# Operands of the delta chain beside the inverses, last merge in two quadrants, first chunk of the RWKV-7 chain in buffers of its own

## The reference, cut to what matters

```python
# RWKV-7, from a zero state, 8 heads of 64
sa = einsum('bhij,bhj->bhi', s, -kkt)
s = s * wt[:, :, None, :] + sa[..., None] * (kkt * at)[:, :, None, :] + vt[..., None] * kt[:, :, None, :]
y = einsum('bhij,bhj->bhi', s, rt)

# gated delta rule, chunked, from a zero state, 4 heads of 128
tv = triangular_solve(ia, bc[..., None] * vc); tk = triangular_solve(ia, (bc * exp(G))[..., None] * kc)
qk = where(incl, einsum('nbhtd,nbhsd->nbhts', qc, kc) * dmat, 0.0)
u = tvi - tki @ s;  o = (qi * exp(gi)) @ s + qki @ u;  s = exp(gl) * s + (ki * exp(gl - gi)).T @ u
```

## Time and profile before

| | |
|---|---|
| runs | 2246.23 us median (2241.65 to 2248.21) |
| profiled execution | 2248.08 us, its span 2246.0 us, mean granted clock of TensorE 0.934 |
| TensorE matmul busy | 2029.4 us (90%) |
| VectorE, ScalarE, GpSimd busy | 1214.4, 497.2, 222.2 us |
| even inverses and RWKV-7 chain | from 320.4 to 383.9 us, and from 384.4 to 466.1 us |
| delta inverses and delta chain | from 1469.0 to 1505.7 us, and from 1506.2 to 1554.1 us |

### The profile page before, as it was taken

One profiled execution on the slowest core, in us unless ns is written; L12 is line 12 of the kernel. 1 busy time (PEld: TensorE's weight loads), 2 busy tenths in 40 slices (PEclk: granted clock), 3 DMA queues, 4 the chain that ended last, 5 costly groups with the idle time before them and its releaser, 6 DMA issues. The chain is left out here.

```text
span 2246.0 us, 40426 instructions
## 1 busy us (share of the span) xinstructions
PE 2029.4 (90%) x17833; PEld 1887.6 (84%) x17833; DVE 1214.4 (54%) x1490; ACT 497.2 (22%) x833; POOL 222.2 (10%) x217
## 2 busy tenths in 40 slices
PE   7998558969988999999999989776699799999999
PEld 6997448859976999999999965465599589999999
DVE  6884655258534655554467445444584355555532
ACT  2221533233222211111011035430422321111000
POOL 3111021013010100000110011011220010000000
PEclk9998767889999999999999989777899999999999
DMA  5221100013562222232222240200244722222321
GB/s 183 86 76 61 38 20 3 1 45 118 171 256 109 94 86 92 93 111 92 79 81 92 93 145 19 84 2 10 99 151 141 299 67 94 93 85 93 109 90 64
DMA packets 52400, 209.10 MB, mean 93 GB/s; under 512 B 6450, under 2 KB 7090, under 8 KB 46258
## 3 DMA queue, kind: packets, MB, share of 16 engines
q1 hardware_dynamic: 52274, 207.30, 26.9%
HBM read 193.88 MB, written 13.40 MB: 92 GB/s over the span
## 5 line engine op out<-in xcount | busy, mean ns | idle before, releaser
L416 PE MATMUL ps<-mx_hi,w_hi 128*128 128x260 f32 x2560 | 521.1, 285 | 16.9 <-DVE w_lo L393 9.7
L416 PE MATMUL ps<-mx_hi,w_lo 128*128 128x260 f32 x2560 | 516.9, 284 | 0.0
L416 PE MATMUL ps<-mx_lo,w_hi 128*128 128x260 f32 x2560 | 516.6, 283 | 0.0
L416 PEld LDWEIGHTS ps<-mx_hi,w_hi 128*128 128x128 f32 x2560 | 396.3, 189 | 21.3 <-DVE w_lo L393 9.9
L416 PEld LDWEIGHTS ps<-mx_hi,w_lo 128*128 128x128 f32 x2560 | 396.3, 189 | 0.0
L416 PEld LDWEIGHTS ps<-mx_lo,w_hi 128*128 128x128 f32 x2560 | 395.4, 189 | 0.0
L391 DVE CAST w_hi<-w 128x1024 fp32r<-128x1024 f32 (+1 forms) x256 | 187.9, 734 | 309.7 <-PE ps L416 302.6
L393 DVE TENSOR_TENSOR w_lo<-w,w_hi 128x1024 fp32r<-128x1024 f32 (+1 forms) x256 | 330.4, 1290 | 8.8
L416 PE MATMUL ps<-hid_hi,w_hi 128*128 128x260 f32 x704 | 141.8, 283 | 0.0
L416 PE MATMUL ps<-hid_hi,w_lo 128*128 128x260 f32 x704 | 141.7, 283 | 0.0
L416 PE MATMUL ps<-hid_lo,w_hi 128*128 128x260 f32 x704 | 141.3, 282 | 0.0
(11 more groups left out here) (490 smaller groups left out, 2834.1 us busy)
## 6 DMA issues: line engine op xcount, KB each, us to landing
w<-in_w_gu SPq DMA_DIRECT2D x88, 512.0 KB, 3.3
w<-in_w_in SPq DMA_DIRECT2D x56, 512.0 KB, 3.3
w<-in_w_down SPq DMA_DIRECT2D x32, 704.0 KB, 4.0
w<-in_w_xkv SPq DMA_DIRECT2D x32, 512.0 KB, 3.4
scr<-in_mem_k SPq DMA_DIRECT2D x10, 1024.0 KB, 6.9
scr<-in_mem_v SPq DMA_DIRECT2D x10, 1024.0 KB, 14.1
w<-in_w_out SPq DMA_DIRECT2D x16, 512.0 KB, 3.3
w<-in_w_xq SPq DMA_DIRECT2D x16, 512.0 KB, 3.4
```

Source lines behind the costliest of these rows:

```text
L416: ins = nc.tensor.matmul(self.ps[:, 2 * (o % 2) + s, 0:b - a], w[:, k, :], v[:, x, a:b], start=first, stop=last)
```

## The change

1. **Delta inverses.** A new class `ChainOperands` does there, in PSUM banks 4 to 7, what the delta chain opened with: TensorE turns the values after `fill` (16 transposes), turns the keys after merge 0 (16 transposes), multiplies keys by queries after merge 2 (16 products). ScalarE copies the turned values (chunks 0 and 1 ahead of merge 0, 2 and 3 behind it), VectorE scales the turned keys after merge 1 (4 instructions) and the products after merge 3 (4 instructions).
2. **Delta chain.** What is left ahead of the first product is the scaling of the inverses by beta, now in two halves. GpSimd scales `k` and then `q` by the decay, both from the stage's start. The copy of the first right side is gone; the scratch offsets are laid out anew.
3. **Last merge.** In TensorE's order L1670 of group n-2 alternates, head by head, with L1663 of group n. With four groups that is two steps with both, with two groups none.
4. **RWKV-7 chain.** Even chunks use what were the odd buffers, cleared by GpSimd in the inverses' stage (`zeroed`); the others are cleared by VectorE behind the masked copies of chunk 0. Chunk 0's transposes and matrices have banks of their own. The two products with the zero state (L1836 and L1869 for t = 0) are left out.

```diff
-    E_INV, E_VT, E_KT, E_QK, E_U, E_S, E_R = 6144, 0, 2048, 4096, 8192, 10240, 12800
+    E_INV, E_VT, E_KT, E_QK, E_U, E_S, E_R = 6144, 8192, 10240, 13408, 0, 3584, 12288
+class ChainOperands:
+    def bank(self, t):
+        return self.k.ps[:, 4 + t, :].rearrange("p (h e) -> p h e", h=4)
+    def keys_turned(self, pe):
+        k = self.k
+        for t in range(NC):
+            pe.wait_ge(k.chain_kept.sem, k.chain_kept.at(t + 1))
+            for h in range(4):
+                ins = k.nc.tensor.transpose(self.bank(t)[:, h], self.keys[:, h, t * P:(t + 1) * P], k.const("ident"))
+            ins.then_inc(k.chain_turned.sem, 1)
+    def keys_scaled(self, dve):
+        k = self.k
+        for t in range(NC):
+            dve.wait_ge(k.chain_turned.sem, k.chain_turned.at(NC + t + 1))
+            decay = self.decay[:, t].unsqueeze(2).to_broadcast([P, 4, P])
+            k.dve.tell(k.nc.vector.tensor_tensor(self.kt[:, t], self.bank(t), decay, ALU.mult), k.chain_scaled)
...
 unit_inverses, TensorE:
                     fill(pe, g, 2 * g)
+                if beside:
+                    beside.values_turned(pe)
...
+                    if beside and n == 0:
+                        beside.keys_turned(pe)
+                    if beside and n == 2:
+                        beside.keys_by_queries(pe)
...
+                for n in range(groups + 2):
+                    first, second = n < groups, n >= 2
...
+                        if first:
+                            ins = nc.tensor.matmul(self.ps[upper, 2 * n, cols], lt[n][lower, h, upper], wide[n][lower, h],
+                                                   start=True, stop=True)
...
+                        if second:
+                            ins = nc.tensor.matmul(self.ps[lower, 2 * n - 3, cols], wide[n - 2][upper, h],
+                                                   inv[n - 2][upper, h, upper], start=True, stop=True)
...
 unit_inverses, GpSimd, ScalarE, VectorE:
+                for t in zeroed:
+                    self.pool.step(nc.gpsimd.memset(t, 0.0))
...
+                if beside:
+                    beside.values_kept(act, range(0, 2))
...
+                    if beside and n == 0:
+                        beside.values_kept(act, range(2, NC))
...
+                    if beside and n == 1:
+                        beside.keys_scaled(dve)
+                    if beside and n == 3:
+                        beside.products_scaled(dve)
...
 rwkv_chain:
+        def token_bank(t, n):
+            return 6 + n % 2 if t else n
+        def matrix_bank(t, n):
+            return 6 if t else 6 - 2 * n
...
-                for out in (ak, rb, rk):
-                    for half in out:
-                        self.dve.step(nc.vector.memset(half, 0.0))
                 self.dve.step(nc.vector.memset(st[:, 0], 0.0))
                 for n in range(3):
                     masked(0, n)
+                for out in (ak, rb, rk):
+                    self.dve.step(nc.vector.memset(out[1], 0.0))
...
 delta_chain, TensorE in the loop, GpSimd, VectorE:
+                        if t == 1:
+                            pe.wait_ge(self.pool_out.sem, self.pool_out.at(1))
...
+                        ins = nc.tensor.matmul(self.ps[:, 5, h * P:(h + 1) * P], inv[:, t, h], rr[:, h] if t else vt[:, 0, h],
+                                               start=True, stop=True)
...
+                for x in (k, q):
+                    self.pool.tell(nc.gpsimd.tensor_tensor(x[:, :, 0:T], x[:, :, 0:T], eg[:, :, 0:T], ALU.mult), self.pool_out)
...
+                for g in range(2):
+                    own = inv[:, 2 * g:2 * g + 2].rearrange("p c h t -> p (c h) t")
+                    beta = col[:, 1, 2 * g:2 * g + 2].rearrange("p c h -> p (c h)").unsqueeze(2).to_broadcast([P, 8, P])
+                    ins = nc.vector.tensor_tensor(own, own, beta, ALU.mult)
+                    self.dve.step(ins) if g else self.dve.tell(ins, self.vector_out2)
```

More of the change, by code:

```diff
@@ L1570, in _, with unit_inverses @@
                 self.dve.tell(nc.vector.tensor_tensor(ss, ss, t2, ALU.add), self.vector_out)
-    def unit_inverses(self, groups, factor, lt_at, uv_at, x_at, ltd_at, xd_at, inv, fill):
+    def unit_inverses(self, groups, factor, lt_at, uv_at, x_at, ltd_at, xd_at, inv, fill, beside=None, zeroed=()):
         nc = self.nc
@@ L1658, in _ @@
                     ins.then_inc(self.tensor_out2.sem, 1)
-                for g in range(groups):
-                    pe.wait_ge(*after(self.vector_out, 2 + n_merge, g))
-                    pe.wait_ge(*after(self.scalar_out2, 0, g))
-                    for h in range(8):
[L1663 to L1672, removed]
+                for n in range(groups + 2):
+                    first, second = n < groups, n >= 2
+                    if first:
+                        pe.wait_ge(*after(self.vector_out, 2 + n_merge, n))
+                        pe.wait_ge(*after(self.scalar_out2, 0, n))
+                    if second:
+                        pe.wait_ge(*after(self.scalar_out, 2 + n_merge, n - 2))
+                        pe.wait_ge(*after(self.pool_out, 2, n - 2))
+                    for h in range(8):
+                        cols = slice(64 * h, 64 * h + 64)
+                        if first:
+                            ins = nc.tensor.matmul(self.ps[upper, 2 * n, cols], lt[n][lower, h, upper], wide[n][lower, h],
+                                                   start=True, stop=True)
+                            if h == 7:
+                                ins.then_inc(self.tensor_out.sem, 1)
+                        if second:
+                            ins = nc.tensor.matmul(self.ps[lower, 2 * n - 3, cols], wide[n - 2][upper, h],
+                                                   inv[n - 2][upper, h, upper], start=True, stop=True)
+                            if h == 7:
+                                ins.then_inc(self.tensor_out2.sem, 1)
                 self.tensor_out.count += (1 + n_merge + 2) * groups
@@ L1829, in _ @@
                         j = h % 4
[L1830 to L1831 removed]
+                        ins = nc.tensor.matmul(self.ps[:, h // 4, j * 64:(j + 1) * 64], ak[x][:, h], vt[x][:, j, h // 4],
+                                               start=j == 0, stop=not t and j == 3, skip_group_check=True)
                     if t:
                         pe.wait_ge(self.vector_out2.sem, self.vector_out2.at(t))
[L1834 to L1837, removed]
+                        for h in self.BY_ROWS:
+                            rows, j = self.head_slot(h)
+                            ins = nc.tensor.matmul(self.ps[:, h // 4, j * 64:(j + 1) * 64], A[rows, j, cols], st[rows, t, j],
+                                                   start=False, stop=j == 3, skip_group_check=True)
                     ins.then_inc(self.tensor_out.sem, 1)
+                    if not t:
+                        pe.wait_ge(self.vector_out.sem, self.vector_out.at(3))
                     for h in range(8):
@@ L1864, in _ @@
                     for h in range(8):
-                        nc.tensor.matmul(out_of(t, h), sa[:, h], rb[x][:, h], start=False, stop=False, skip_group_check=True)
+                        ins = nc.tensor.matmul(out_of(t, h), sa[:, h], rb[x][:, h], start=False, stop=not t and h % 4 == 3,
+                                               skip_group_check=True)
+                    if not t:
+                        ins.then_inc(self.tensor_out.sem, 1)
                     prepare(t + 1, (4,))
[L1867 to L1871, removed]
+                    if t:
+                        for h in self.BY_ROWS:
+                            rows, j = self.head_slot(h)
+                            ins = nc.tensor.matmul(out_of(t, h), st[rows, t, j], R[rows, j, cols], start=False, stop=j == 3,
+                                                   skip_group_check=True)
+                        ins.then_inc(self.tensor_out.sem, 1)
                     prepare(t + 1, (5,))
@@ L2972, in _ @@
             def _(act):
-                act.wait_ge(self.tensor_out.sem, self.tensor_out.at(1))
-                self.act.tell(nc.scalar.activation(wide(vt), self.banks(0, 4), ACT.Copy), self.scalar_out)
                 for t in range(NC):
```

104 lines of the change are left out of this document (54 added, 50 removed).

## The result

The changed kernel's median is **2219.62 us** (2216.16 to 2224.28, four runs) against 2243.95 (2241.65 to 2248.21, four runs): ratio 0.9889, 95% interval 0.9871 to 0.9906. It is 24.3 us faster; 21.8 were forecast, and 2224.4 lies 4.8 above the median, within the range. Of the 4.8, 2.3 are the kernel before itself: the forecast started from its median of 2246.23, here it is 2243.95. The profiled execution took 2224.28, span 2222.1, so against the span of before 23.9 us shorter.

A forecast was written before the change was run, and what follows sets the result against it. It saw small TensorE products at half clock and waits at the openings of both chains as the bound. Even 3.2 + 7.9 + 8.0 = 19.1, delta 10.3 - 7.6 = 2.7, together 21.8 saved: 2224.4 us, range 2218 to 2237.

The forecast's parts named there:

- Last merge: Even inverses: 64x64 products in two quadrants overlap, two steps save 3.2 us (bounds 0 to 3.4).
- Rival 3: Last merge of even inverses: the quadrants don't overlap, 3.2 us less saved, 2227.6 us; chance 0.08.
- Opening: RWKV-7 chain: gapless transposes and matrices, clock rising 5.3 us after their start; first real product 7.9 us earlier.
- Rival 1: RWKV-7 chain: the clock doesn't rise early; total saving 14.5 us, 2231.7 us; chance 0.26.
- Chunk 0: RWKV-7 chain: full clock and one zero product less give 15.1 instead of 23.1 us, 8.0 saved.
- Delta inverses: Work moved there from the delta chain costs 7.6 us, between 6 and 10 (L1663 wholly at half clock).
- Delta opening: Delta chain: GpSimd scales first, VectorE stands still meanwhile; first state copy still ends 10.3 us earlier.
- Rivals 2 and 4: Delta chain: VectorE gets the port first, 2219.9 us, chance 0.12; or GpSimd issues both scalings first, 2228.2 us, chance 0.05.
- rival 2: Delta chain: VectorE gets the port before GpSimd, state copy 4.5 us earlier still, 2219.9 us; chance 0.12.
- The sum: Whole kernel: even mixer saves 19.1 us and delta pair 2.7, together 21.8.
- Rival 5: RWKV-7 chain: TensorE's clock stays low throughout, 11.5 us slower, 2257.7 us; chance 0.04.

The follow-up runs named there:

- e1: Kernel before with only the new order of the last merge; 2241.03 us, ratio 0.9982 to before.
- e2: Kernel before with only the new RWKV-7 chain (own buffers and banks, no zero products, memsets on GpSimd); 2229.68 us, ratio 0.9948.
- e7: Changed kernel with GpSimd's scalings of k and q moved into the delta inverses; 2216.43 us, ratio 0.9879 to before.
- e5: Kernel before with 2, 7 and 4 unread products of constants in TensorE's waits ahead of chunk 0's three matrices; 2239.67 us, ratio 0.9979.
- e6: Changed kernel with GpSimd waiting until VectorE has scaled both halves by beta in the delta chain; 2217.68 us, ratio 0.9886 to before.
- the fillers: Unread products of constants in TensorE's waits, added to e8 ahead of both last merges and in the delta chain; 2208.68 us, ratio 0.9842 to before.
- e8: e7 with the four scalings of the key-query products one merge earlier, behind merge 2; 2213.26 us, ratio 0.987 to before.
- e3: Kernel before with only the two delta parts (inverses and chain); 2241.23 us, ratio 0.9992 to before.

## Why the prediction was right, point by point

- **Last merge** (forecast 3.2, measured 4.6; 4.4 in e1). Right in kind, undersized twice. I took 2.0 us for a step with both, by L1635's spacing; it is 1.7, an exact halving, 24 records in a window against 12, 3.4 in two steps. The Trainium skill (TensorE: Matmul & The Clock Gate, Part 3) has products of different row groups overlap, and by that rule I had given 3.4 too; the trace agrees with the overlap, but not with starts about 4 ns apart: the records of the two quadrants start 0.04 to 0.06 us apart (373.24, 373.30, 373.34, 373.40 in the changed kernel). The other 1.0 to 1.2 is the rise of the clock at 376.9, which the forecast did not have. Rival 3 is out.
- **Opening** (7.9, measured 8.6). The structure came as written: first real product 5.92 into the stage, forecast 6.6. The clock rose 3.5 us after the first transpose (380.16 to 383.7), not 5.3; behind it lay the twelve transposes and more than half of the first matrix. Other profiles have 3.1 (e2) and 4.0 (e7). I had worked the 5.3 out from a stretch with one kind of product; it was too late by 1.8. The mean of 0.84 that I gave for it doesn't place the rise, since the clock fell again within those five microseconds; windows of one microsecond do (0.67 from 325 to 326, so 325.7). Rival 1 is out.
- **Chunk 0** (8.0, measured 7.5). Length 15.56 against 15.1. The wait for the third mask, which I costed at nothing behind a L1830 of 3.6 us, showed 0.44. The step contradicted itself: it took L1830 at half clock, while the same forecast had the full clock by then, at which that product is 2.0 long. The untouched chunk 0 took 22.12 in e1 and 23.26 in e3, so the gain is 6.6 to 7.7, depending on the profile. L1869 and the memsets cost nothing, as said. e5 shows that the rest is the clock.
- **Delta inverses** (7.6, measured 7.1). From fill: merge 0 starts 0.2 earlier (forecast 0), merge 1 a further 1.9 later (forecast 1.9 for keys and 0.2 for ScalarE), merge 2 no later (0), merge 3 3.6 later (3.8), the last merge 1.4 (1.7), and the way to the stage's end 0.4: L1745 runs at half clock throughout, where L1663 had full clock for its first sixteen records. I had that as a bound, with a total of 10; it happened and cost 0.4. It isn't due to the change either: in e1 the untouched L1663 starts at half clock too. Against the commoner profile of before the sum is 5.6, below my lower bound of 6, and nearly all of the difference is in the keys: merge 1 comes 6.9 behind merge 0, against 5.0 in the profile that I had and 6.2 in the commoner one, where the clock fell. So they cost 1.9 or 0.7. I could not see that from one profile.
- **Delta opening** (10.3, measured 10.7). GpSimd came first by 0.01 us, VectorE's first half showed some 5.6, the first product 5.61 in (5.8), the state copy ended at 11.7 (12.1). GpSimd's two scalings took 9.95, against 9.11 in e6 where they ran apart from VectorE's: room for VectorE's first half between them, as forecast, though 0.8 and not 1.2. Rivals 2 and 4 did not occur, and e6 shows that rival 2's order is worth 4.3 at the first product. The Trainium skill (SBUF - State Buffer, section on who interferes with whom) calls this an exclusive lock for the whole instruction; 11.02 against 2.49 agrees.
- **The sum.** 19.1 forecast for the even mixer, 20.3 measured; 2.7 for the delta pair, 3.6 measured, 3.1 against the other profiles. Nothing was given back later: all else is +0.1. What I left out is the 2.3 us that the changed chain loses behind the first state when its clock falls; it was in the profile of before too, so the difference of the two hid it. That is luck, and so is an "all else" of +0.1; the parts by themselves are off by 0.3 to 1.4. Rival 5 is out: chunks 1 to 3 are unchanged (16.02, 16.09 and, up to the next stage's first product, 12.53 us; before 16.09, 16.02 and 12.54).

## What to carry to other kernels

Where TensorE's products are small, take the granted clock of the stretch first: closing gaps between them may pay twice, once for the gap and once for the clock in the work behind it (e5 gained 8.9 us in its stretches and 4.1 in the median by adding work). It may also pay nothing: ahead of the last merge of the even inverses the fillers gave 2.9 and cost 3.0. Two elementwise instructions with both inputs in SBUF, on GpSimd and VectorE at a stage's start, run one after the other; put the one that TensorE waits for first, or GpSimd's into a stage where VectorE works on PSUM (e7). Before a profile's split between stages is trusted, look at the same untouched stage in a second profile.

## What the runs showed of the hardware that was not expected

- The order of VectorE and GpSimd costs VectorE 8.5 us (11.02 against 2.49 for the same two instructions) and GpSimd 0.8 (9.95 against 9.11).
- Pairs of 64x64 products in two quadrants, at half clock, took the clock up 3.7 us after they began (373.2 to 376.9), in e1 4.4 us (373.8 to 378.2, the last 0.8 of them with one product at a time), where in the kernel before the same products one at a time ran from 369.54 to 383 at 0.50.
- The same code in the same stage has two clock courses: the delta pair unchanged shows 29.62 and 24.24 us in one profile and 30.8 and 21.9 in four others. What decides isn't shown; in e6 and e7, which start the first product 4.3 us earlier, the second stretch has no fall of the clock and takes 22.4; in e8, with the same early start, it takes 23.1.
- The rise of the clock in the untouched chunk 0 came 13.4, 15.5 and 15.9 us into it in three profiles (e1, before, e3), so that a chunk 0 of 22.1 and one of 23.3 are the same code.
